# A two-block transformer on one core: expert lists turned by one rounded product per token half, and the first mixer's head norms and rotations set between the units of its pooling branch

## The reference

```python
# first block, layer 0: the mixer
q, k, v, p = project_a(h, w_in_a[e], qk_norm_g[e])    # q, k: RMS norm over each head of 64
q, k = apply_axial_rope(q, tabs), apply_axial_rope(k, tabs)
attn = latent_attention(q, k, v, kc, vc)              # 8 query heads, 2 key heads, 512 keys
x = x + m[:, :, 5] * (concat([attn, multiscale_pool(p, pool_w, pool_scale)]) @ w_out_a)

# second block, in both layers: 16 experts, 2 for each token
scores = sigmoid(t @ router_w)                        # combine: weights of the two chosen
for e in range(16):
    he = silu(t @ w_gate[e]) * (t @ w_up[e])
    y = y + combine[:, e:e + 1] * (he @ w_down[e])
```

## Time and profile before

| | |
|---|---|
| median of 3 runs | 2336.82 us (2333.8 to 2336.99) |
| the profiled execution, its own time | 2338.63 us |
| its span, first to last instruction | 2336.8 us |
| PE busy | 2249.4 us (96%) |
| DVE busy | 1546.5 us (66%) |
| ACT busy | 1093.8 us (47%) |
| mean granted TensorE clock | 0.983 |

### The profile page before, as it was taken

The page is one execution under the profiler, slowest core; times in us unless marked ns, Lnnn a source line. Parts: engine busy times, 40 slices in busy tenths (PEclk is TensorE's granted clock), DMA queues, the critical chain, the costliest instruction groups (busy, mean ns, idle before and its releaser), DMA issues.

```text
span 2336.8 us, 35665 instructions
## 1 busy us (share of the span) xinstructions
PE 2249.4 (96%) x15176; PEld 2038.5 (87%) x15176; DVE 1546.5 (66%) x1683; ACT 1093.8 (47%) x1374; POOL 6.7 (0%) x16
## 2 busy tenths in 40 slices
PE   9999999979999999989999979999999999999998
PEld 7888888758999999979999948899998978899997
DVE  4896696144777777527775443888887443888887
ACT  4221232244334434425434443667776454677775
POOL 0000000000000000000000000000000000000000
PEclk9999999999999999989999989999999989999999
DMA  8577777414887788437885512778886412678885
GB/s 307 199 251 245 253 257 254 169 37 159 308 296 256 264 302 300 171 109 253 302 302 188 181 37 90 271 291 295 296 320 239 155 62 91 248 289 296 312 302 212
DMA packets 126738, 535.49 MB, mean 229 GB/s; under 512 B 11744, under 2 KB 47912, under 8 KB 82416
## 3 DMA queue, kind: packets, MB, share of 16 engines
q1 hardware_dynamic: 124896, 524.33, 62.5%
q0 software_dynamic: 944, 5.72, 0.6%
q10 hardware_dynamic: 736, 3.10, 0.3%
HBM read 532.04 MB, written 1.06 MB: 228 GB/s over the span
## 4 chain that ended last, share of the span: by engine, by line
PE 87%; DVE 6%; ACT 4%; DMA 1%; issue 1%; SPq 0%; DVEq 0%; ACTq 0%
PE PS L878 16%; PE PS L1297 13%; PE PS L804 10%; PE PS L952 9%; PE PS L1331 7%; PE PS L900 7%; PE PS L999 5%; PE PS L839 5%; DVE moe_low L2347 2%; PE PS L1255 2%; PE PS L773 1%; PE PS L1232 1%; PE PS L705 1%; PE PS L940 1%; DMA ring<-mod_w 1%
## 5 line engine op out<-in xcount | busy, mean ns | idle before, releaser
L878 PE MATMUL PS<-h_parts,FFN_HIGH 128*128 128x256 f32 x2112 | 383.1, 284 | 5.0 <-DVE h_parts L1957 5.0
L2347 DVE TENSOR_TENSOR moe_low<-moe_ring,W_HIGH 128x2048 fp32r<-128x2048 f32 x128 | 292.9, 2290 | 79.8 <-ACT W_HIGH L1732 79.8
L878 PEld LDWEIGHTS PS<-h_parts,FFN_HIGH 128*128 128x128 f32 x2112 | 329.0, 192 | 5.8 <-issue 5.5
L878 PE MATMUL PS<-h_parts,ring_low 128*128 128x256 f32 x1056 | 298.7, 283 | 0.0
L1297 PE MATMUL PS<-moe_low,HXH 128*96 128x256 f32 x1008 | 282.5, 280 | 0.0
L1732 ACT ACTIVATE W_HIGH<-moe_ring 128x2048 fp32r<-128x2048 f32 x128 | 244.5, 1912 | 23.0 <-PE PS L1331 21.9
L1984 DVE TENSOR_TENSOR ring_low<-ring,FFN_HIGH 128x2048 fp32r<-128x2048 f32 x99 | 226.6, 2291 | 40.5 <-ACT FFN_HIGH L1528 40.4
L2015 DVE SCALAR_TENSOR_TENSOR roots<-CB,cond_rows,roots 128x1024 f32<-128x1024 f32 x186 | 238.3, 1281 | 10.0 <-DVE roots L2015 0.9
L1528 ACT ACTIVATE FFN_HIGH<-ring 128x2048 fp32r<-128x2048 f32 x99 | 188.8, 1909 | 98.9 <-DMA ring<-down_w 89.5
L878 PEld LDWEIGHTS PS<-h_parts,ring_low 128*128 128x128 f32 x1056 | 202.6, 192 | 0.0
L1297 PEld LDWEIGHTS PS<-moe_low,HXH 128*96 128x96 f32 x1008 | 164.1, 163 | 0.3
(11 more groups left out here) (330 smaller groups left out, 4870.4 us busy)
## 6 DMA issues: line engine op xcount, KB each, us to landing
moe_ring<-moe_w SPq DMA_DIRECT2D x192, 1024.0 KB, 5.0
CB<-mod_rows SPq DMA_DIRECT2D x192, 512.0 KB, 5.9
ring<-up_w SPq DMA_DIRECT2D x88, 1024.0 KB, 5.0
ring<-lin_w SPq DMA_DIRECT2D x55, 1024.0 KB, 4.9
ring<-down_w SPq DMA_DIRECT2D x43, 1024.0 KB, 5.7
CB<-mod_dual SPq DMA_DIRECT2D x96, 128.0 KB, 2.6
ring<-mod_w SPq DMA_DIRECT2D x8, 1024.0 KB, 8.7
CB<-mod_rows SPq DMA_DIRECT2D x32, 128.0 KB, 2.7
```

What stands on the lines that cost most here:

```text
L878: return mm(PS[:, i % 2, h * S:(h + 1) * S], a[:, k, h * P:(h + 1) * P], b[:, k, :], start=start, stop=(k == KT - 1 and j == 2), skip_grou ...
L2347: tt(by_tile(moe_low[:, moe_slot(l, p), :]), by_tile(moe_ring[:, moe_slot(l, p), :]), w_high_tiles(p), ALU.subtract).then_inc(w_low, 1)
```

## The change

**Mixer a.** ACT squares each chunk of `A_QK` right after it has copied it out, and takes the roots of two chunks before it copies unit 3, of the third before unit 4. PE averages chunks 0 and 1 before unit 3, chunk 2 after it, rotates chunks 0 and 1 (`turn_pairs`) before unit 4 and chunk 2 after ACT has copied unit 4. The means go to PSUM banks 4 to 6 and the rotations to banks 2, 3 and 0. The products with `pool_w` and DVE's scaling into `CAT` move into the attention, ahead of the work of r = 2. The wait of ACT for `cat_ready` goes; PE has it at r = 3.

**Expert lists.** `turn_list` makes two fp32r products of 130 columns instead of two transposes and two f32 products. The moving operand (`TURN`, two buffers, laid over `roots`) is the identity with two columns beside it, the rounded weight of each token for this expert and what rounding left. The second product adds its weights into the columns of the first. ACT adds the two sums (a copy, then Identity with a bias) and copies the list from two stretches. DVE makes the rounded weights once in each `route` (`TURN_W`, two steps) and copies four columns for each expert (`place`), for which PE waits (`place_ready`). ACT writes the two identities once.

```diff
-HEAD_NORMS = {"a": (3, 0), "e": (4, 4), "r": (2, 0)}
+HEAD_NORMS = {"a": (3, 4), "e": (4, 4), "r": (2, 0)}
+ROT_BANK_A = (2, 3, 0)
...
+        TURN = rounded("TURN", roots_at, [P, 400])
+        TURN_W = rounded("TURN_W", roots_at + 400 * 4, [P, TT, NE, 2])
+        def turn_side(e, t):
+            first = (e % 2) * (P + 4) + (2 if t == 0 else 0)
+            return TURN[:, first:first + P + 2]
+        def turn_weights(e):
+            first = (e % 2) * (P + 4)
+            return TURN[:, first:first + 2 * (P + 2)].rearrange("p (t c) -> p t c", t=TT)[:, :, 0:2]
...
+                    if which == "a" and r == 2:
+                        behind_two()
+                    if which == "a" and r == 3:
+                        pe.wait_ge(cat_ready, 1)
...
-                by_tokens("a_in", 2, 3, 4)
-                head_norm("a", A_SQ, "mean64")
+                def turn_pairs(c):
+                    at = slice(c * BANK, min((c + 1) * BANK, 5 * S))
+                    pe.wait_ge(hn_ready, c + 1)
+                    mm(PS[:, ROT_BANK_A[c], 0:at.stop - at.start], tab("rot_axial"), A_QK[:, at], start=True, stop=True)\
+                        .then_inc(rot_psum, 1)
+                def p_unit(t):
+                    i = t - 1
+                    arrived(u0 + i)
+                    wait(pe, lin_ready, t - 3)
+                    for j in range(TT):
+                        last = in_products("a_in", i, 0, PS[:, t % 4, j * S:(j + 1) * S], True, slice(j * P, (j + 1) * P))
+                    last.then_inc(unit_done, 1)
+                head_norm("a", A_SQ, "mean64", (0, 1))
+                p_unit(4)
+                head_norm("a", A_SQ, "mean64", (2,))
+                turn_pairs(0)
+                turn_pairs(1)
+                p_unit(5)
+                pe.wait_ge(lin_ready, 6)
...
                 pe.wait_ge(rot_ready, 3)
-                pe.wait_ge(cat_ready, 1)
-                attention("a")
+                def pooled_products():
+                    pe.wait_ge(pool_ready, 2)
+                    for g in range(4):
+                        last = mm(PS[:, 6 + g // 2, (g % 2) * S:(g % 2 + 1) * S], pool_w[:, g, :], A_POOLED[:, g, :],
+                                  start=True, stop=True)
+                    last.then_inc(poolw_psum, 1)
...
-                    words = LIST_WORDS[e // GROUP % 2][:, :, e % GROUP * CAP:(e % GROUP + 1) * CAP]
+                    words = LIST[e // GROUP % 2][:, :, e % GROUP * CAP:(e % GROUP + 1) * CAP]
+                    pe.wait_ge(place_ready, e0 + e + 1)
                     for t in range(TT):
-                        tr(PS[0:CAP, 3, t * P:(t + 1) * P], words[:, t, :], tab("ident"))
-                    for t in range(TT):
-                        last = mm(PS[0:CAP, 3, S:S + 1], words[:, t, :], work[:, 22, t * NE + e:t * NE + e + 1],
-                                  start=(t == 0), stop=(t == TT - 1))
+                        last = mm(PS[0:CAP, 3, t * P:t * P + P + 2], words[:, t, :], turn_side(e, t), start=(t == 0),
+                                  stop=(t == TT - 1), skip_group_check=True)
                     last.then_inc(mo_tpsum, 1)
...
+            def head_root(which, wide, chunks):
+                bank = HEAD_NORMS[which][1]
+                for c in chunks:
+                    w = slice(c * BANK, (c + 1) * BANK)
+                    act.wait_ge(hms_psum, HEAD0[which] + c + 1)
+                    line(af(wide[:, w], PS[:, bank + c, :], ACT.Ln, bias=eps[:, 0:1]))
+                    line.wait()
+                    af(wide[:, w], wide[:, w], ACT.Exp, scale=-0.5).then_inc(hr_ready, 1)
...
             def mixer_a():
-                for t, u in enumerate((0, 1, 2)):
-                    evacuate("a_in", t, u, A_QK[:, t * BANK:(t + 1) * BANK])
+                def square(c):
+                    w = slice(c * BANK, (c + 1) * BANK)
+                    act.wait_ge(lin_ready, c + 1)
+                    af(A_SQ[:, w], A_QK[:, w], ACT.Square).then_inc(hsq_ready, 1)
+                for t in range(3):
+                    evacuate("a_in", t, t, A_QK[:, t * BANK:(t + 1) * BANK])
+                    if t < 2:
+                        square(t)
                 evacuate("a_in", 3, 2, A_V[:, :, :])
-                for t, u in ((4, 3), (5, 4)):
-                    evacuate("a_in", t, u, A_P[:, :, (t - 4) * S:(t - 3) * S])
-                act.wait_ge(lin_ready, 6)
-                head_norm("a", A_QK, A_SQ, A_R)
+                square(2)
+                head_root("a", A_R, (0, 1))
+                evacuate("a_in", 4, 3, A_P[:, :, 0:S])
+                head_root("a", A_R, (2,))
+                evacuate("a_in", 5, 4, A_P[:, :, S:2 * S])
                 act.wait_ge(pool_psum, 1)
                 for c in range(2):
                     af(A_POOLED[:, 2 * c:2 * c + 2, :], PS[:, 4 + c, :].rearrange("p (g n) -> p g n", g=2),
                        ACT.Copy).then_inc(pool_ready, 1)
-                act.wait_ge(cat_ready, 1)
                 attention("a")
...
-                    af(PLACE_W[0:CAP, e % 2:e % 2 + 1], PS[0:CAP, 3, S:S + 1], ACT.Copy).then_inc(mo_tready, 1)
+                    rest_w = small[0:CAP, 28 + e % 2:29 + e % 2]
+                    line(af(rest_w, PS[0:CAP, 3, P + 1:P + 2], ACT.Copy))
+                    turned_list = PS[0:CAP, 3, 0:2 * (P + 2)].rearrange("p (t n) -> p t n", t=TT)[:, :, 0:P]
+                    af(LIST_T[0:CAP, e % 2, :].rearrange("p (t n) -> p t n", t=TT), turned_list, ACT.Copy)
+                    line.wait()
+                    af(PLACE_W[0:CAP, e % 2:e % 2 + 1], PS[0:CAP, 3, P:P + 1], ACT.Identity, bias=rest_w)\
+                        .then_inc(mo_tready, 1)
...
+                if l == 0:
+                    for b in range(2):
+                        af(TURN[:, b * (P + 4) + 2:b * (P + 4) + 2 + P], tab("ident"), ACT.Copy)
...
+                    if which == "a" and r == 2:
+                        behind_two()
...
+                dve.wait_ge(ld_late, LATE)
...
+                rotation("a", A_QK, 5 * S, A_SQ, A_R, "cos_axial", "sin_axial", ROT_BANK_A)
+                def pooled():
+                    dve.wait_ge(poolw_psum, 1)
+                    for g in range(4):
+                        last = ts(CAT[:, 4 + g, :], PS[:, 6 + g // 2, (g % 2) * S:(g % 2 + 1) * S],
+                                  cols[:, COL["pool_scale"].start + g:COL["pool_scale"].start + g + 1], None, ALU.mult)
+                    last.then_inc(cat_ready, 1)
+                attention("a", pooled)
...
+                weights = by_token(w(22))[:, ::-1, :]
+                step(dve.tensor_copy(TURN_W[:, :, :, 0], weights))
+                step(tt(TURN_W[:, :, :, 1], weights, TURN_W[:, :, :, 0], ALU.subtract))
...
+                def place(e):
+                    if e0 + e >= 2:
+                        dve.wait_ge(mo_tpsum, e0 + e - 1)
+                    dve.tensor_copy(turn_weights(e), TURN_W[:, :, e, :]).then_inc(place_ready, 1)
...
+                place(0)
                 for d in range(KT):
...
                     split(MOE_AT[e, 0] + 3)
+                    if e + 1 < NE:
+                        place(e + 1)
                     gated(e, 1)
```

More of the change, by code:

```diff
@@ L398, in program @@
                              "mo_silu", "mo_g"))
+        place_ready = sem("place_ready")
         mo_gtpsum, mo_gthigh, mo_gtready, mo_yhigh, mo_y = (
@@ L1007, in out_proj, with head_norm @@
                 keep_busy(n, 8)
-            def head_norm(which, sq, mean):
+            def head_norm(which, sq, mean, chunks=None):
                 n, bank = HEAD_NORMS[which]
-                for c in range(n):
+                for c in chunks or range(n):
                     pe.wait_ge(hsq_ready, HEAD0[which] + c + 1)
@@ L1022, in rotation, with attention @@
                         .then_inc(rot_psum, 1)
-            def attention(which):
+            def attention(which, behind_two=None):
                 first = 0 if which == "a" else 16
                 for r in range(11):
+                    if which == "a" and r == 2:
+                        behind_two()
+                    if which == "a" and r == 3:
+                        pe.wait_ge(cat_ready, 1)
                     if r < 8:
@@ L1099, in mixer_a @@
                 last.then_inc(pool_psum, 1)
-                pe.wait_ge(pool_ready, 2)
-                for g in range(4):
-                    last = mm(PS[:, 6 + g // 2, (g % 2) * S:(g % 2 + 1) * S], pool_w[:, g, :], A_POOLED[:, g, :],
-                              start=True, stop=True)
-                last.then_inc(poolw_psum, 1)
-                pe.wait_ge(hn_ready, 3)
-                rotation(A_QK, 5 * S, "rot_axial")
-                pe.wait_ge(rot_ready, 3)
-                pe.wait_ge(cat_ready, 1)
-                attention("a")
+                pe.wait_ge(rot_ready, 3)
+                def pooled_products():
[4 more added lines that the diff above has]
+                    last.then_inc(poolw_psum, 1)
+                attention("a", pooled_products)
```

(17 more changed lines are left out.)

4 lines of the change are left out of this document (2 added, 2 removed).

## The result

The changed kernel takes 2323.85 us (median of 5 runs, 2321.69 to 2324.77), the kernel before 2336.99 beside it. The ratio is 0.9947, its 95% interval 0.9935 to 0.9959. That is 13.1 us less where 20.9 were forecast, inside the range.

The account below looks back on a forecast made before the run. PE was taken as the bound, busy for 2249.4 of 2336.8 us. Pooling branch 8.7 less, attention 0.8 less, lists 12.6 less and stage starts 1.2 more gave 20.9 less than 2336.82, so 2316 us; range 2312.5 to a microsecond above 2325.

Parts of the forecast that it names:

- the forecast alone: Whole kernel: the main case without rivals, 2316 us, within 2313 to 2319.5; chance 0.55.
- slow short products: Expert lists, rival: a short rounded product goes at plain f32 pace, a list gains 0.12, 2325 us; chance 0.25.
- Mixer a up to the attention: First pooling unit to first scores: PE's new order takes 22.9 us against 31.63, 8.7 less.
- The slack given to ACT's roots: Pooling branch: some 4.5 us of ACT work for chunks 0 and 1 stays covered until needed after unit 3.
- The attention: Mixer a's attention: full clock gains 0.95, CAT scalings delay r = 2, r = 3 begins earlier; 0.8 us less.
- The rival with half clock at the start: Mixer a's attention still starts at half clock: 0.2 to 1.3 us lost, 2317 to 2318.1; chance 0.13.
- The lists: Expert lists: the product pair takes 0.14, so 0.42 us less for each of 30 lists, 12.6 less.
- the rival at 2325: Expert lists: short rounded products at plain f32 pace, the pair taking 0.44 us; chance 0.25.
- PE stands still behind it: Expert lists: the first list of either stage gives nothing, as PE waits for DVE's low parts (0.96 and 1.03).
- The start of a stage: Before the first HXL: three more DVE instructions of 0.19 cost 0.6 us a stage, 1.2 more in all.
- The chance of 0.93 for faster: Whole kernel: the first three of five cases are faster by more than 4.7 us; same 0.04, slower 0.03.
- the two large terms: Mixer a up to the attention, 8.7 us less, and the expert lists, 12.6 us less.

Follow-up runs that it names:

- e4_fill: e3_pad with 8 f32 filler products put into PE's 2.33 us wait in mixer a's attention, ahead of the transposes of r = 3; 2317.27 us (0.9911).
- e7_moved: e3_pad with the two steps that make TURN_W and the first place taken behind DVE's third gather of each stage; 2322.53 us (0.9929).
- e10_all: e9_late_fill with the move of e7_moved; 2315.45 us (0.9913).
- e3_pad: The changed kernel with 16 more f32 products, never run, in the skipped branch of moe0; 2319.7 us (0.9924).
- e5_stop: The kernel before with 36 f32 products, never run, in the skipped branch of moe0, moving its target to 179; 2342.05 us (1.0016).
- e2_lists: The kernel before with the lists' part of the change alone, mixer a as before; 2329.72 us (0.9972).
- e6_late: e3_pad with attention a's pool_w products moved to r = 8 and 9 and the scalings into CAT behind the attention; 2319.49 us (0.992).
- e9_late_fill: e6_late with six f32 filler products ahead of the scores of r = 2, where PE waits 1.53 us; 2317.63 us (0.9926).
- e8_both: e4_fill and e7_moved in one; 2317.49 us (0.9914).

## Why the prediction was right, and where its terms were off

The number is right in part by luck. 2323.85 lies outside the 2313 to 2319.5 that I gave the forecast alone, and inside the range only because that was drawn up to 2326 for slow short products, a case that did not come about.

**Mixer a up to the attention** was right: 8.6 of 8.7, and the one wait named there was 0.69 where I had 0.9. The slack given to ACT's roots held.

**The attention** was wrong by 1.8. The step that failed is "From there on the loop is a chain of scores, maxima, exponentials and copies through three engines, with the same order in both kernels, and I let it run equally". The order is the same, but the loop did not run equally. The larger part is the clock: I had it at 1.00 throughout, with nothing for a fall inside the loop, and PE's wait of 2.33 us was followed by one. With that wait filled (e4_fill) the attention takes 1.56 less, 35.08, which is 0.46 under the old 35.54. The rest, 0.3, is the choice of the member. I had computed that r = 2 would begin 0.4 later than in the old run (measured 0.1), and r = 3 0.8 earlier (1.2), and took the second number. r = 4 waits for the exponentials of r = 2 and for the copies queued behind them on ACT, so the first number counts: in e4_fill its maxima begin 13.57 behind the first score, in the old run 13.54. The rival with half clock at the start did not come about; the clock fell 11 us later.

**The lists** were right in mechanism: no penalty for a rounded product of 130 columns, so the rival at 2325 falls by the 0.15 for the pair. By the Trainium skill (TensorE: Matmul & The Clock Gate, section LDWEIGHTS) the pair would take 0.16, an estimate; the row's 0.15 is between that and the 0.14 that I took. The term was too large by 2.6 of 12.6. The pair costs 0.17 with what it does to the next product, so 0.39 for a list, and 0.36 to 0.43 is measured from list to list (21.07 to 20.71; 19.68 to 19.75 against 19.31 and 19.32 in the last three). The first list of the second group of four experts and that of the third gain 0.18 only (21.54 to 21.36), since PE waits longer for DVE's `HXL` in that expert; compare these two rows, the old and the new:

```profile
1566.07 0.52 PE L1314 MATMUL PS<-tabs,SG 96*128 96x96 f32 x4 [0.28 <-DVE HXL L2353]
```

```profile
1556.80 0.52 PE L1351 MATMUL PS<-tabs,SG 96*128 96x96 f32 x4 [0.45 <-DVE HXL L2428]
```

And the 16th gains 0.2 at most, as PE then waits for DVE's `SG` ahead of the last expert's transposes, 0.86 us instead of 0.65 (both in moe0). I had applied the rule "PE stands still behind it" to the first list of a stage alone.

**The start of a stage** costs 0.39 and 0.37 instead of 0.6 (e7_moved, e10_all: three instructions moved away give it back whole). The delay arrived whole, as I had it, but its price was too high: I had 0.19 for each instruction, and by the rows above the three put the first `HXL` 0.39 later behind the last routing step (0.62 instead of 0.23). From the last routing step on, the starts are 0.11, 0.21, 0.22 and, of `HXL`, 0.08 apart.

**What was missing** is the stop of PE: no part of the forecast looked at where PE's own instructions come from. Of the +3.7 behind the last list of moe0 it is 2.7, and the half clock behind it, which e3_pad has without a stop, 1.3; the 16th list takes the rest off. e3_pad and e5_stop show that the stop depends on the place of the code and on nothing else that the change does.

What PE waits for is in the packets of the instruction queue. There are 123 of them in the run, 16 KB each, one for some 250 records of PE (30,590 with its weight loads and waits); DVE and ACT have about 2,000 records each, so the queue must be PE's. For 1788.6 to 1789.7, in the middle of the stop, the view of the DMA queues has one:

```profile
q8 instruction: 1, 0.02, 5.3%
```

By the trace it runs from 1788.66 to 1789.59, and PE's ninth product starts at 1790.88, 1.29 behind its end. In e2_lists the packet ends 1.40 ahead of that product, and in e5_stop 1.32, though the three stops are 4.21, 2.25 and 4.62 long: the stop ends about 1.3 behind the packet, whenever that comes. In the nine profiles without a stop a packet comes there too, but it starts only after the ninth product has begun. So PE stood because its next instructions had not arrived. Why the packet comes no sooner with the target at this place, no run shows.

Together: +0.1 pooling branch, +1.8 attention, +2.6 lists, -0.4 starts, +3.7 behind the last list of moe0 and -0.8 spread make 7.0, and -20.9 + 7.0 = -13.9, as by the spans; the medians have 13.1. The chance of 0.93 for faster was well placed, as the two large terms were bounded by rows; the number was off by what hangs on them further down.

## What to carry over

When a change moves the start of a loop over several engines, follow the latest of its first members through each in-order queue, not the average or the last; and look at each wait that comes into the open for what the clock does behind it, as a few filler products can be cheaper than the wait. In a long straight-line program with skipped branches, a stop with no releaser just behind a branch is worth one test with padding in the skipped part, and a look at the packets of the instruction queue, before it is charged to the edit. What such a stop costs is how much later the next stage starts, not its own length. Gains per repetition have to be taken off wherever the engine waits before the next repetition ends, not only at the first.

## What the runs showed of the hardware

- PE's stop without a releaser just behind a skipped branch: 4.21, 2.25 and 4.62 us with the target at 179, 178 and 179 instructions modulo 256 of PE's program, each behind the eighth product past the target, and each over 1.3 to 1.4 us behind the end of a 16 KB packet on PE's instruction queue; none with the target at 35, 36, 243, 244, 19 and 12. Other places were not tried, so the width of the bad stretch stays open, and so does the modulus: a period of 128 would fit the same kernels.
- The granted clock fell to half at a wait of 1.53 us in e6_late and stayed at 1.00 behind one of 1.37 in e9_late_fill. It does not follow from the wait alone: at the 1.53 us wait for `SG` behind the last scatter of moe0 it fell in three of nine profiles (e3_pad, e4_fill, e10_all), and at the two waits at the start of moe0 (0.96 or 1.34, then 1.03) in three of twelve (e5_stop, e7_moved, e8_both).
- A rounded product of 130 columns with 96 of stationary operand goes at 0.07 to 0.08 us, the pace of its loading, with nothing added for being short.
